# In-projection of a hybrid layer: seven half-size products for a pair of column tiles

## The reference

```
h    = rms_norm(x, attn_norm_g)
proj = h @ w_in                        # 1024 x 3600: q 512, k 256, v 256, z 1024, xbc 1536, dt 16
q, k, v, z, xbc, dt = split(proj)
attn = dilated_attention(rms_norm per head of q and k, v)
xbc  = silu(causal_depthwise_conv(xbc, 4 taps) + b)
y    = ssd(xs * softplus(dt + bias), ...) + d_skip * xs
y    = rms_norm(y * silu(z), ssm_norm_g)
x    = x + concat(attn, y) @ w_out
x    = x + conv_ffn(x)                 # up-projection, 3 taps, gate, down-projection
x    = x + sigmoid(rms_norm(x) @ w_gate) * (p @ w_proj)
```

## Time and profile before

| | |
|---|---|
| runs | 3037.71, 3038.43, 3032.75 us |
| profiled execution | 3039.24 us, its span 3037.5 us |
| granted clock, mean | 0.983 |
| PE busy | 2920.8 us (96%), 14755 instructions |
| DVE busy | 1999.2 us (66%) |
| ACT busy | 1140.1 us (38%) |
| POOL busy | 282.2 us (9%) |
| in-projection | the first 681.6 us of the span |

### The profile page before, as it was taken

How to read it: one execution, slowest core, us unless ns; L and a number is a source line. 1 busy time by engine, 2 the same in 40 slices (tenths; PEclk the granted TensorE clock), 3 DMA queues, 4 the chain that set the end, 5 groups by cost and what they waited for, 6 DMA issues and landing times. The chain is left out here.

```text
span 3037.5 us, 38641 instructions
## 1 busy us (share of the span) xinstructions
PE 2920.8 (96%) x14755; PEld 2306.0 (76%) x14818; DVE 1999.2 (66%) x2492; ACT 1140.1 (38%) x1734; POOL 282.2 (9%) x278
## 2 busy tenths in 40 slices
PE   7999999998989999899999999899999999999999
PEld 5778887884657566688778888788888788877887
DVE  7334555117565754545698899889998786776743
ACT  5322121212435353312255544544444444444321
POOL 0000000003444433000001000000000000000000
PEclk9999999998999999999999999999999999999999
DMA  3551222228674764633322234425543766443632
GB/s 140 181 188 56 75 70 63 87 73 211 190 202 145 189 170 120 209 128 129 140 104 84 97 139 155 185 84 194 194 153 104 248 206 221 150 158 116 191 114 67
DMA packets 260124, 435.02 MB, mean 143 GB/s; under 512 B 44049, under 2 KB 128529, under 8 KB 252913
## 3 DMA queue, kind: packets, MB, share of 16 engines
q1 hardware_dynamic: 255570, 408.32, 42.6%
q0 software_dynamic: 4384, 24.41, 2.1%
HBM read 312.18 MB, written 120.00 MB: 142 GB/s over the span
## 5 line engine op out<-in xcount | busy, mean ns | idle before, releaser
L103 PE MATMUL up_banks<-up_x_hi,up_w_hi 128*128 128x512 f32 x1232 | 484.4, 393 | 23.7 <-DVE up_x_lo L2683 8.5
L104 PE MATMUL up_banks<-up_x_lo,up_w_hi 128*128 128x512 f32 x1232 | 482.2, 391 | 0.0
L105 PE MATMUL up_banks<-up_x_hi,up_w_lo 128*128 128x512 f32 x1232 | 482.1, 391 | 0.0
L103 PE MATMUL inp_ps<-inp_h_hi,carry_q 128*128 128x512 f32 x896 | 355.6, 397 | 18.5 <-DVE inp_h_lo L202 9.8
L104 PE MATMUL inp_ps<-inp_h_lo,carry_q 128*128 128x512 f32 x896 | 351.7, 393 | 0.0
L105 PE MATMUL inp_ps<-inp_h_hi,carry_k_two 128*128 128x512 f32 x896 | 351.5, 392 | 0.0
L103 PEld LDWEIGHTS up_banks<-up_x_hi,up_w_hi 128*128 128x128 f32 x1232 | 233.0, 189 | 79.1 <-issue 15.9
L105 PEld LDWEIGHTS up_banks<-up_x_hi,up_w_lo 128*128 128x128 f32 x1232 | 232.9, 189 | 49.1
L104 PEld LDWEIGHTS up_banks<-up_x_lo,up_w_hi 128*128 128x128 f32 x1232 | 233.1, 189 | 48.3 <-issue 0.2
L2724 DVE SCALAR_TENSOR_TENSOR carry_rows<-carry_squares,up_conv_w,carry_rows 128x1024 f32<-128x1024 f32 x176 | 232.1, 1319 | 24.4 <-ACT carry_rows L2555 19.5
L103 PE MATMUL down_banks<-down_x_hi,down_w_hi 128*128 128x512 f32 x616 | 241.2, 391 | 7.0 <-DVE down_x_lo L2195 7.0
(11 more groups left out here) (378 smaller groups left out, 5317.6 us busy)
## 6 DMA issues: line engine op xcount, KB each, us to landing
carry_room<-in_w_up_dram SPq DMA_DIRECT2D x84, 512.0 KB, 4.4
act<-carry_rows SPq DMA_DIRECT2D x44, 512.0 KB, 2.9
carry_room<-cum_rows SPq DMA_DIRECT2D x16, 1024.0 KB, 6.6
carry_room<-x SPq DMA_DIRECT2D x7, 2048.0 KB, 9.0
carry_room<-in_w_in_dram SPq DMA_DIRECT2D x26, 512.0 KB, 6.0
xbc<-carry_room SPq DMA_DIRECT2D x12, 1024.0 KB, 5.7
carry_room<-xbc SPq DMA_DIRECT2D x16, 768.0 KB, 4.3
down_x<-act SPq DMA_DIRECT2D x12, 1024.0 KB, 8.2
```

Of the source, the lines that this page charges most:

```text
L103: pe.matmul(out, w_hi, x_hi, start=first, stop=False, skip_group_check=onto)
L104: pe.matmul(out, w_hi, x_lo, start=False, stop=False, skip_group_check=onto)
L105: return pe.matmul(out, w_lo, x_hi, start=False, stop=last, skip_group_check=onto)
```

## The change

The eight gates and twelve mixer inputs become ten pairs in two rounds (`InOrder`: pairs 0, 1, 8 and 9 are gates, 2 to 7 mixer inputs; RING = 5). q and k stay as they are. Values and time steps follow them at once, in blocks of 512 tokens in the order 2, 3, 1, 0 (`V_ORDER`), so that the places of blocks 2, 3 and half of 1 in `h_hi` and `h_lo` come free for the sums of token blocks of the first round. For the second round SP reads five token blocks of x again, each when its old content has had its last product. ACT multiplies by the norm gain, DVE and POOL make the sums, ACT and DVE split them.

An eviction no longer multiplies by `rstd`: it adds bank and copy into `pre`. POOL multiplies `pre` by `rstd` (`scale`, 1024 tokens); then ACT makes the first tap (`first_tap`) or the gate's Silu, DVE three taps, ACT the Silu. POOL also makes the third weight difference (`s3`) and the third token sum (`third`), and keeps the last three tokens of the first round for the second (`halo`). The loops of the engines are gone: 140 steps are written out. `UpOrder` moves up in the file unchanged. In the next stage POOL waits for all stores of this one before it sets its state to zero, and the values lose a column of ones.

```diff
+class InOrder(UpOrder):
+    RING = 5
+    PAIRS = (NT1 - XBC0) // 2
+    def column(self, j, b):
+        z = {0: 0, 1: 1, self.PAIRS - 2: 2, self.PAIRS - 1: 3}
+        return Z0 + 2 * z[j] + b if j in z else XBC0 + 2 * (j - 2) + b
...
+        def last_of(g, b):
+            return place[g, S4] if b else place[g, A22]
+        ended = {}
+        for g in range(G):
+            for b in range(2):
+                ended.setdefault(last_of(g, b), []).append((g, b))
...
+            def load_x(r, v):
+                if r == 0:
+                    sp.wait_ge(v_mm, 6 if v == A22 else 2)
+                else:
+                    sp.wait_ge(mm, done(PAIRS - 1, v))
...
+            def third(r):
+                at = part(h_raw, r, S3)
+                pool.wait_ge(x_made, MADE[r, S2])
...
+                pool.tensor_tensor(at, part(h_raw, r, S2), part(h_hi, r, A11).bitcast(F32), ALU.subtract).then_inc(x_third, 1)
+                pool.wait_ge(x_third, 2 * r + 1)
+                pool.tensor_tensor(at, at, part(h_lo, r, A11).bitcast(F32), ALU.subtract).then_inc(x_third, 1)
+            def scale(g, b):
+                r = g // PAIRS
+                blk = pre[b][:, 3:3 + HALF]
...
+                for c in (c11_s, c12_s) if b else (c21_s, c22_s):
+                    pool.wait_ge(c, g + 1)
+                pool.tensor_tensor(blk, blk, norm.rstd[:, r * HALF:(r + 1) * HALF], ALU.mult).then_inc(ready[b], 1)
...
+            for i in range(V - 2):
+                store_values(i)
+            s3(0)
+            s3(1)
+            third(0)
...
+            for s in range(len(steps)):
...
+                if s == again + 10:
+                    third(1)
+                for g, b in ended.get(s, []):
+                    scale(g, b)
...
+            for s in range(len(steps) + 5):
...
+                elif v in (A11, S2, S3):
+                    take(g, v)
+                weights(s + RING)
...
+                if s in (again + 3, again + 5):
+                    w = A11 if s == again + 3 else A12
+                    scaled(1, w)
+                    token_high(1, w)
...
+                for e, b in ended.get(s - 4, []):
+                    if convolved(e):
+                        silu(e, b)
+                for e, b in ended.get(s - 1, []):
+                    first_tap(e, b) if convolved(e) else gate(e, b)
...
+            weights(3)
+            weights(4)
+            fourth(0)
+            values(7)
+            for s in range(len(steps) + 3):
+                g, v = steps[s] if s < len(steps) else (None, None)
+                for e, b in ended.get(s - 2, []):
+                    if convolved(e):
+                        convolve(e, b)
...
+                elif v == S3:
+                    evict(g, S1)
+                elif v in (A22, S4):
+                    evict(g, v)
+                    if v == A22 and g not in firsts:
+                        evict(g, A12)
+                weights(s + RING)
...
+            for s, (g, v) in enumerate(steps):
+                pe.wait_ge(wlo, s + 1)
...
+                if v == S2:
+                    pe.wait_ge(p1c_s, g + 1)
+                if v == S3:
+                    pe.wait_ge(u2c_s, g + 1)
+                if v == A12 and g >= 2:
+                    pe.wait_ge(c11_s, g - 1)
...
+                if v == S4:
+                    pe.wait_ge(c22_s, g + 1)
...
+                for q in range(Q):
+                    if q == 1 and s in (0, 2):
+                        turn(V - 2 + s // 2)
...
+                    last = three_passes(pe, bank(g, v), ring_hi[s % RING][:, c], ring_lo[s % RING][:, c], at_hi[:, q], at_lo[:, q],
+                                        q == 0 and v not in (S2, S3, S4), q == Q - 1, v in (S2, S3, S4))
+                last.then_inc(mm, 1)
```

More of the change, by code:

```diff
@@ L264, in in_projection @@
                   dt_raw, dt_bias, a_log, cum_rows, e_rows, norm_rows):
     QKT = (ATTN + KVH * HD) // P
+    order = InOrder()
+    steps, place, done, RING, PAIRS = order.steps, order.place, order.done, order.RING, order.PAIRS
+    firsts, seconds = order.firsts, order.seconds
+    A11, S1, S2, A12, S3, A22, S4 = range(7)
+    G, HALF, Q = order.ROUNDS * PAIRS, 1024, KD // 2
+    V = 2 * NB
+    V_ORDER, V_BANKS, DT_BANKS = (2, 3, 1, 0), (1, 2, 0, 4, 6, 5, 3, 7), (1, 2, 3, 0)
     with Phase(nc, "inp") as ph:
@@ L317, in in_projection, with part, half_of, column @@
         block = ph.block()
+        def part(h, r, v):
+            half, blk = {A11: (0, 0), A12: (1, 0), S1: (0, 2), S2: (1, 2), S3: (0, 3), A22: (0, 1), S4: (1, 3 if r else 1)}[v]
+            return h[:, half * Q:half * Q + Q, blk * 512:(blk + 1) * 512]
+        def half_of(v):
+            return 0 if v in (A11, S1) else 1
+        def column(g, b):
+            return order.column(g % PAIRS, b)
+        def convolved(g):
+            return order.convolved(g % PAIRS)
+        def nth(g):
+            return order.nth(g)
@@ L356, in _ @@
                     spread_inverses(t - 2)
[L358 to L367, removed]
-                             ).then_inc(stored[b], 16)
@@ new lines, in _ @@
+            spread_inverses(QKT - 2)
+            load_raw(0)
+            spread_inverses(QKT - 1)
+            load_raw(1)
+            for v in (S1, S2, A22):
+                load_x(0, v)
+            readers = {order.read(g) - RING: g for g in range(G - 2)}
+            for s in range(len(steps) + 6):
+                if s in readers:
+                    load_raw(readers[s] + 2)
+                for n, v in ((1, A11), (3, A12), (5, S1), (7, S2), (11, A22)):
+                    if s == again + n:
+                        load_x(1, v)
+                if s == len(steps) - 2:
+                    sp.wait_ge(mm, len(steps) - 2)
@@ L477, in gate @@
[L477 to L489 removed]
+                act.wait_ge(sum_done, t + 1)
@@ L508, in _ @@
-            for b in range(2):
-                for n in range(NB):
-                    blk = slice(n * 512, (n + 1) * 512)
-                    act.wait_ge(evacuated, NT1 - 2 + b * NB + n + 1)
-                    act.activation(stage[b][:, blk], stage[b][:, blk], ACT.Silu).then_inc(part_out, 1)
+            scaled(0, S1)
+            values(1)
+            scaled(0, S2)
+            values(2)
+            weights(0)
+            values(3)
+            token_high(0, S1)
+            values(4)
@@ L588, in _ @@
+            for t in range(QKT):
                 b = t % 2
@@ L3179, in program @@
     mix_t = scratch("mix_t", (ATTN + INNER, SEQ))
[L3180 removed]
+    v_tok = [scratch(f"v_tok{n}", (SEQ, 2 * HD)) for n in range(2)]
     y_root = scratch("y_root", (1, SEQ))
```

746 lines of the change are left out of this document (522 added, 224 removed).

## The result

The changed kernel took 3096.75 us (median of 4 runs, 3093.4 to 3098.7), the kernel before it 3037.14 (4 runs, 3032.8 to 3038.4): a ratio of 1.0198, 95% interval 1.0180 to 1.0215. It is slower by 60 us, outside the forecast range of 2998 to 3063. The spans of the profiled executions are 3097.0 and 3037.5 us, 59.5 apart.

What follows compares the result with a forecast made beforehand. TensorE alone was taken to bound the rewritten in-projection stage. -54.4 + 24 + 22 + 11 + 4 = +6.6 us on 3039.2 gave 3045.8, stated as 3045 us, range 2998 to 3063.

Steps and rivals of the forecast that it cites:

- TensorE's saving: In-projection tiles 8 to 27: 1680 matmuls in place of 1920, 240 x 0.2267 = -54.4 us if TensorE never waits.
- Convolution groups: Mixer-input groups: POOL and DVE exclude each other, so 21.5 us a group against TensorE's 19.04; +24 us.
- each weight pair is asked for 16 us ahead of its first use: Extra weight and x loads in the rewritten stage: hidden, SP only having to issue within that lead; costed at nothing.
- the forecast's own formula: Convolution groups: 2 x (0.8 + 4 x 2.5), and 2.5 for the last of round two; +24 us.
- Change of rounds: Passage from round one to two, token blocks made on the spot: +22 us, bounds 8 and 28.
- Most of it fits: Change of rounds: ACT's, DVE's and POOL's token work mostly fits beside the surrounding gates without taps.
- four waits: Change of rounds: second S2's copy 3 to 4 us, pair 9's S1 eviction 4, pair 11's A12 about 11, new S2 3.
- Start: Time steps, values and first token sums at the stage's start: +11 us, bounds 3 and 16.
- the turn: Last value tile in step 2: its eviction stands behind DVE's two-input work beside POOL's third sum; 8 us.
- End: Last eviction, POOL scaling, Silu and larger store before the next stage: +4 us, bounds 3 and 6.
- (a): Rival: the port is not the bound, POOL's pieces fall into DVE's idle time; 3007 us, chance 0.38.
- (c): Rival: the change of rounds runs away, POOL's third sum interleaving with DVE's long passes; 10 to 20 more, 3060 us, chance 0.12.

Runs made afterwards that it cites:

- e9_both: Changed kernel with stores ahead of loads, first tap behind the copy of S2, and POOL's scaling cut to 8 of 1024 columns: 19.05 us a group.
- e4_order: Changed kernel with only queue order altered: SP's stores ahead of weight loads, ACT's second first tap behind the copy of S2; 22.7 us less, groups 20.4 us.
- e10_tokens: Changed kernel with reordered queues, third sum on DVE, weights taken later, and round two's token blocks cut to 8 of 512 columns: change of rounds loses 15.7 us.
- e1: Changed kernel with POOL's scaling cut to 8 of 1024 columns, the rest left out: 3067 us, groups 20.85 us.
- e3_third: Changed kernel with both passes of the third token sum moved from POOL to DVE: 5.2 us less at pair 2, 5.3 in the change of rounds.
- e11_start: e8_all with the first two time rows and the third and fourth value evictions moved earlier in DVE's queue: 3045.5 us.
- e2_dummy2: Changed kernel with POOL's scaling cut to 8 columns, plus an idle POOL multiplication nobody waits for in round two: 3071.3 us.
- e5_scale: Changed kernel with the scaling and the copies of three columns moved from POOL to DVE: groups 22.3 us.
- e8_all: Changed kernel with reordered queues, later weights, norm-weight scaling fused into DVE's subtractions, and POOL's stage arithmetic on DVE: groups 20.3 us, change of rounds 34.2.

## Why the prediction was wrong

*TensorE's saving*, -54.4: right; e9_both shows the rate.

*Convolution groups*, 24 against 40: the mechanism and the chain were right, the failed step is "each weight pair is asked for 16 us ahead of its first use ... SP ... only has to be within that lead". SP's queue holds stores as well as loads. A store ready at 384.9 stood 4.8 us behind a load's wait, and the next tap stood at the store. That is 2.1 us a group, costed at nothing (e4_order, which moves a tap in ACT's queue too). The exclusion itself was sized too high: DVE's own sum was put at 21.5 a group and is 20.4 (e4_order): 16.0 plus 4.1 of lengthening (low parts 1.4, L1023 1.8, taps 0.9) and 0.2 to 0.3 of waits, where 5.3 were added for POOL, since POOL falls partly beside evictions and waits. That the forecast length of 21.5 came within 1 us of the 22.5 is luck: two errors partly cancelled. The 1 us makes 9 of the 16 us that are missing (3.5 in place of 2.5 in the forecast's own formula gives 33); the other 7 no run takes apart.

*Change of rounds*, 22 with bounds 8 and 28 against 44: mis-sized by a factor of two. "Most of it fits" failed: ACT's and DVE's token work was put at nothing but for four waits (which add to 21 or 22 as listed, not to 22 to 24), and those grew from 3 or 4, 4 and 3 to 11.1, 8.1 and 7.3. The nearest row, the up-projection's 15 us, is close to what e10_tokens leaves (15.7) when the token work is taken away; the 25 us of that work stood on top. The third sum behind POOL is 5.3, the scaling on POOL 9 to 13 (e1, e9), ACT standing at weights about 5 by subtraction; these overlap, so they are not a sum. Here again the 16 us were counted to TensorE's use, while ACT rounds the weights five steps (13.6 us) ahead, in order, with its copies and gates behind.

*Start*, 11 against 22.8: the turn, forecast 8, cost 7.1, and with the slow matmuls behind it (2.6), a gap at 304 us (1.5) and its own matmuls (2.2) nearly all of the 14.0 at pair 2; e3_third takes 5.2 of them. The 2.2 are work that only changed its place, so ahead of the first weight step 11.0 were lost where 3 were forecast: this is the part of the term that failed. DVE's standing at the key block's landing (11.6 us in the trace) looked like the cause; e11_start moved the evictions past it and gained nothing ahead of the first weight step. Which queue sets this part stays open.

*End*, 4 against 6.8: within a little of its bounds (3 and 6); no run took it apart.

*Rivals.* (a), 0.38, was refuted by e2_dummy2, though the exclusion cost a group less than forecast (4.1 us against 5.3). The slower side's (c), 0.12 at 3060, named the place but not the amount. Each of the four terms lay above its upper bound. The common reason: each was the lateness of one chain followed, with every queue otherwise on time. The Trainium skill's rule cited in the prediction ("SBUF — State Buffer", "Who interferes with whom") held for the whole instruction: 5.0 us for a low part beside a 4.6 us pass. An eviction, one input in SBUF, stayed at 0.68 (at 502.72, beside a POOL pass of 6.6 us). The taps' 0.9 us a group come from POOL's weight difference and not from the scaling: their mean is 1.43 us in the changed kernel, in e1_thin and in e5_scale alike, and 1.28 in e8_all, where POOL has nothing.

## What to carry to other kernels

Before a change that brings a second engine close to the first one's time (here 20.4 against 19.04 us a group), follow every in-order queue, the DMA-issuing one too: for each wait in it, name what stands behind. Count a transfer's lead to its first reader on any engine, not to the matmul. And where work is packed into a transition, compare each engine's sum there with the time of the transition alone; the nearest rows of a like transition without that work are a floor, not an estimate.

## What the runs showed of the hardware

DVE's low part started at 255.79, 0.03 us before POOL's pass, and still ended only behind it, after 5.0 us. By the printed starts it was first; as POOL's spans are rough, 0.03 us don't decide it. POOL's spans stretch too: its pass took 6.59 us at 500.68 where DVE had started a 2.28 us two-input instruction 0.16 us earlier, against 4.62 at 255.82, and a difference of 128x512 took 2.26 us beside taps against 1.27 us alone (at 557.42). A copy of three columns took 0.53 us on POOL in round one and 0.65 to 1.19 in round two, and 0.16 to 0.17 on DVE; the scaling of 128x1024 took 2.0 to 2.45 and 1.23 (median).
